# Both attention branches of the second mixer on split fp32r operands, with a smaller key window for one of them and its bias table built elsewhere

## The reference

```python
def neighbourhood_attention(q, k, v, k_ctx, v_ctx, rpb):
    ...
    c0 = np.clip(cols - kc // 2, 0, GRID_W - kc)
    col_idx = (c0[:, None] + np.arange(kc)[None, :]).astype(np.int32)
    ...
        bias = rpb[:, row_off[:, None, None], col_off[None, :, :]].transpose(0, 2, 1, 3)
        s_loc = jnp.einsum('bwhd,brwchd->bhwrc', q_r, k_nb) + bias.astype(q.dtype)
        s_ctx = jnp.einsum('bwhd,bnhd->bhwn', q_r, k_ctx)
        s = jnp.concatenate([s_loc.reshape(B, H, GRID_W, kr * kc), s_ctx], axis=-1)
        p = jax.nn.softmax(s.astype(jnp.float32), axis=-1).astype(q.dtype)
    ...
def gqa_attend(q, k, v):
    s = jnp.einsum('btkgd,bskd->bkgts', q, k)
    p = jax.nn.softmax(s.astype(jnp.float32), axis=-1).astype(q.dtype)
    return jnp.einsum('bkgts,bskd->btkgd', p, v)
```

## Time and profile before

| | |
|---|---|
| median of 3 runs | 3286.6 us (3282.76 to 3290.73) |
| profiled execution, its own time | 3282.52 us |
| its span | 3280.8 us |
| mean granted clock of TensorE | 0.878 |
| busy: PE | 2668.0 us (81%) |
| busy: DVE | 2247.1 us (68%) |
| busy: ACT | 1519.0 us (46%) |
| busy: POOL | 301.4 us (9%) |

### The profile page before, as it was taken

The page is one execution under the profiler, slowest core; times in us unless marked ns, Lnnn a source line. Parts: engine busy times, 40 slices in busy tenths (PEclk is TensorE's granted clock), DMA queues, the critical chain, the costliest instruction groups (busy, mean ns, idle before and its releaser), DMA issues. The chain is left out here.

```text
span 3280.8 us, 38147 instructions
## 1 busy us (share of the span) xinstructions
PE 2668.0 (81%) x12972; PEld 2125.4 (65%) x12972; DVE 2247.1 (68%) x2162; ACT 1519.0 (46%) x1375; POOL 301.4 (9%) x263
## 2 busy tenths in 40 slices
PE   2957965489994499479978359999999999999991
PEld 2844635377773399446657347777787877877771
DVE  5566656378785411356542579999999999999985
ACT  2222120167672323124432136777677776777760
POOL 0100000023321000000000000011111011111110
PEclk9985557599997699789999569999999999999995
DMA  5613511289994322020021159999999999999994
GB/s 205 232 30 141 167 26 59 104 323 371 362 383 172 103 65 95 24 46 1 1 103 52 53 208 355 369 366 359 366 371 366 368 354 366 371 367 366 359 352 147
DMA packets 261961, 732.14 MB, mean 223 GB/s; under 512 B 34995, under 2 KB 75122, under 8 KB 261810
## 3 DMA queue, kind: packets, MB, share of 16 engines
q1 hardware_dynamic: 237394, 654.41, 55.3%
q0 software_dynamic: 19872, 72.39, 5.8%
q10 hardware_dynamic: 4608, 4.20, 0.4%
HBM read 693.16 MB, written 37.80 MB: 223 GB/s over the span
## 5 line engine op out<-in xcount | busy, mean ns | idle before, releaser
L48 PE MATMUL psum_all<-sb_ring_r,sb_arena_r 128*128 128x512 f32 (+1 forms) x2912 | 1071.2, 368 | 0.0
L152 DVE TENSOR_TENSOR sb_ring_r<-sb_ring,sb_hi_ring 128x2048 fp32r<-128x2048 f32 x297 | 674.2, 2286 | 278.8 <-ACT sb_hi_ring L143 273.2
L47 PE MATMUL psum_all<-sb_hi_ring,sb_arena_r 128*128 128x512 f32 (+1 forms) x1880 | 664.8, 354 | 58.0 <-DVE sb_ring_r L152 55.1
L49 PE MATMUL psum_all<-sb_hi_ring,sb_arena_r 128*128 128x512 f32 (+1 forms) x1880 | 659.5, 351 | 0.0
L143 ACT ACTIVATE sb_hi_ring<-sb_ring 128x2048 fp32r<-128x2048 f32 x297 | 564.2, 1914 | 119.4 <-DMA sb_ring<-in_w_gu_dram 36.4
L48 PEld LDWEIGHTS psum_all<-sb_ring_r,sb_arena_r 128*128 128x128 f32 x2912 | 557.4, 191 | 91.6
L152 DVE TENSOR_TENSOR sb_ring_r<-sb_ring,sb_arena_r 128x2048 fp32r<-128x2048 f32 x258 | 581.8, 2283 | 31.0 <-ACT sb_arena_r L143 30.8
L143 ACT ACTIVATE sb_arena_r<-sb_ring 128x2048 fp32r<-128x2048 f32 x258 | 486.2, 1915 | 198.3 <-DMA sb_ring<-in_w_gu_dram 194.0
L47 PEld LDWEIGHTS psum_all<-sb_hi_ring,sb_arena_r 128*128 128x128 f32 x1880 | 359.5, 191 | 114.8 <-DVE sb_ring_r L152 55.7
L47 PE MATMUL psum_all<-sb_arena_r 128*128 128x512 f32 x1032 | 415.2, 402 | 11.9 <-DVE sb_ring_r L152 6.9
L49 PE MATMUL psum_all<-sb_arena_r 128*128 128x512 f32 x1032 | 412.0, 399 | 0.0
(11 more groups left out here) (311 smaller groups left out, 2879.6 us busy)
## 6 DMA issues: line engine op xcount, KB each, us to landing
sb_ring<-in_w_gu_dram SPq DMA_DIRECT2D x272, 1024.0 KB, 6.8
sb_ring<-in_w_dn_dram SPq DMA_DIRECT2D x136, 1024.0 KB, 9.5
sb_ring<-in_w_e_gate_dram SPq DMA_DIRECT2D x36, 1024.0 KB, 7.4
sb_ring<-in_w_e_up_dram SPq DMA_DIRECT2D x36, 1024.0 KB
sb_ring<-in_w_e_down_dram SPq DMA_DIRECT2D x36, 1024.0 KB, 8.1
sb_ring<-in_w_in_dram SPq DMA_DIRECT2D x27, 1024.0 KB, 5.8
sb_ring<-in_w_mod_dram SPq DMA_DIRECT2D x24, 1024.0 KB, 5.8
sb_arena<-in_w_ada_dram POOLq DMA_DIRECT2D x16, 1024.0 KB, 5.6
```

The costliest lines, as they stand in the source:

```text
L47: eng.matmul(out, a[0], b[0], start=start, stop=False)
L48: eng.matmul(out, a[0], b[1], start=False, stop=False)
L49: return eng.matmul(out, a[1], b[0], start=False, stop=stop)
L152: dve.tensor_tensor(s.lo[c % SLOTS], s.raw[c % SLOTS], s.hi[c % len(s.hi)].bitcast(F32), ALU.subtract).then_inc(s.lo_made, 1)
```

## The change

The new function `attend` replaces `attention` for both branches of the second mixer. Heads are now the inner loop: a unit is still one tile of 128 queries and one head, but the 8 heads of a tile follow one another (4 tiles, 32 units in each branch).

- Token order: `turn(..., order=to_grid)` writes the second mixer's tokens in 4 strips of 16 grid columns by 8 rows; `from_grid` brings the result back. A tile of queries is one strip, so NA needs only the strip and its neighbours: 256 grid keys for the outer tiles 0 and 3 (with context 512 in all), 384 for tiles 1 and 2 (640 in all).
- Operands: scores are fp32r products over 128 rows. NA has three (q_hi by k_hi, q_lo by k_hi, q_hi by k_lo), with queries padded by zeros to 128 rows and keys of two heads stacked. GQ has q_hi stacked over q_lo in 128 rows, and two products. Queries and keys are no longer turned in stages tq, tk and tkc but as the `first` fills of `attend`.
- Probabilities are not scaled. They are turned, ACT makes the rounded half (`rounded`), DVE the rest (`rest`, PSUM minus the half), and PE multiplies both by the values: these hold hi and lo beside each other, 128 columns, so a unit has two matmuls of 128 columns for each of its key blocks, and the result is token-major. `put`, once in 4 units, adds the two parts and multiplies by the inverse sums; `o` fills turn a whole tile, from which `rounded` and `rest` write the halves for the output projection. Stage so is gone.
- The bias table: `setup` stores the padded `rpb`; in mod1 ACT issues 128 DMAs from DRAM to DRAM, one for each query position, each of 64 rows of 192 bytes; in `gates_and_lru` SP loads them (1.57 MB) and a mask, POOL adds the mask in 40 `tensor_tensor` of 128 elements on 128 partitions, and SP stores the table (2.6 MB); NA loads it. Stage nb is gone.
- `rotate_heads` works on all 8 heads at a time and ACT makes a second copy of each tile.

The diff at its core:

```diff
+        @block.scalar
+        def _(act):
+            for p in range(P):
+                first = RPB_PAD + (WIN_R - 1 - p // 16) * RPB_C + (WIN_C - 1 - p % 16) - 16
+                src = bass.AP(k.rpb_pad.tensor, first, [[RPB_R * RPB_C, NH], [RPB_C, GRID_H], [1, 48]])
+                act.dma_start(k.rpb_rows[p], src).then_inc(k.rpb_rows_stored, 16)
...
+            pool.wait_ge(s.rows_loaded, 32)
+            for w, first in enumerate((16, 0, 16, 32, 16)):
+                for h in range(NH):
+                    pool.tensor_tensor(table[:, w, h], rows[:, GRID_H * h:GRID_H * (h + 1), first:first + 16],
+                                       wide(window[:, w], 1, GRID_H), ALU.add).then_inc(s.masked, 1)
...
+            sp.wait_ge(k.rpb_rows_stored, 16 * P)
+            sp.dma_start(k.ring[:, 0:2, :].rearrange("p a n -> p (a n)")[:, 0:NH * GRID_H * 48],
+                         k.rpb_rows.rearrange("p m c -> p (m c)")).then_inc(s.rows_loaded, 16)
+            sp.dma_start(k.ring[:, 5, 0:80], a["window_mask"].rearrange("p w c -> p (w c)")).then_inc(s.rows_loaded, 16)
+            sp.wait_ge(s.masked, 5 * NH)
+            sp.dma_start(k.rpb_table, k.ring[:, 2:5, :].rearrange("p a n -> p (a n)")[:, 0:NH * 5 * P]).then_inc(s.table_stored, 16)
+            sp.wait_ge(s.table_stored, 16)
...
+            def fill(m, srcs):
+                if m >= 2:
+                    pe.wait_ge(s.split, m - 1)
+                for i, src in enumerate(srcs):
+                    ins = pe.transpose(k.psum[:, 4 + m % 2, i * P:(i + 1) * P], src, k.ident[:])
+                ins.then_inc(s.turned, 1)
...
+            def score(u):
+                t = u // 8
+                if u % 8 == 0:
+                    hooks.queries_ready(pe, t)
+                    if "queries" in tiles[t] and t > 0:
+                        pe.wait_ge(s.split, at["q", t, 1] + 1)
+                if u == 0 and first:
+                    pe.wait_ge(s.split, len(first))
+                if u >= 2:
+                    pe.wait_ge(s.exp_done, u - 1)
+                for cols, lhs, rhs, start, stop in tiles[t]["products"](u % 8):
+                    ins = pe.matmul(logits[:, u % 2, cols], lhs, rhs, start=start, stop=stop)
+                ins.then_inc(s.scored, 1)
...
+            def turn_probs(u):
+                pe.wait_ge(s.exp_done, u + 1)
+                for i, (g0, g1) in enumerate(parts(u)):
+                    fill(at["p", u, i], [probs[:, u % 2, g * P:(g + 1) * P] for g in range(g0, g1)])
+            def mix(u):
+                pe.wait_ge(s.split, at["p", u, len(parts(u)) - 1] + 1)
+                q = u // 4
+                if u == 0:
+                    hooks.values_ready(pe)
+                if u % 4 == 0 and q >= 2:
+                    pe.wait_ge(s.put, 2 * (q - 1))
+                dst = k.psum[:, 6 + q % 2, (u % 4) * P:(u % 4 + 1) * P]
+                values = tiles[u // 8]["values"](u % 8)
+                for g, v in enumerate(values):
+                    pe.matmul(dst, hi[:, u % 2, g * P:(g + 1) * P], v, start=g == 0, stop=False)
+                    ins = pe.matmul(dst, lo[:, u % 2, g * P:(g + 1) * P], v, start=False, stop=g == len(values) - 1)
+                ins.then_inc(s.mixed, 1)
...
+            for m, group in enumerate(first):
+                fill(m, group["src"])
+            for u in range(STEPS):
+                if u < NU:
+                    score(u)
+                if prepared(u) is not None:
+                    t = prepared(u)
+                    for i in range(2):
+                        fill(at["q", t, i], tiles[t]["queries"](i)["src"])
+                if 1 <= u <= NU:
+                    turn_probs(u - 1)
+                if turned_out(u) is not None:
+                    t = turned_out(u)
+                    pe.wait_ge(s.o_ready, 2 * t + 2)
+                    fill(at["o", t], [otok[:, t % 2, j * P:(j + 1) * P] for j in range(4)])
+                if 2 <= u <= NU + 1:
+                    mix(u - 2)
...
+            def rounded(m, dst, src):
+                act.wait_ge(s.turned, m + 1)
+                act.activation(dst, src, ACT.Copy).then_inc(s.rounded, 1)
+            def exp(u):
+                act.wait_ge(s.max_ready, u + 1)
+                if u >= 2:
+                    act.wait_ge(s.turned, at["p", u - 2, len(parts(u - 2)) - 1] + 1)
+                if u >= 8:
+                    act.wait_ge(s.inverted, u // 4 - 1)
+                n = tiles[u // 8]["n"]
+                act.activation(probs[:, u % 2, 0:n], logits[:, u % 2, 0:n], ACT.Exp, bias=neg_max[:, u % 2:u % 2 + 1],
+                               accum_out=total[:, u % 8:u % 8 + 1]).then_inc(s.exp_done, 1)
...
+            hooks.act(act)
+            for m, group in enumerate(first):
+                rounded(m, group["hi"], bank(m, group["hi"].shape[-1]))
+            for u in range(STEPS):
+                if u < NU:
+                    exp(u)
+                hooks.act_step(act, u, s)
+                if prepared(u) is not None:
+                    for i in range(2):
+                        m = at["q", prepared(u), i]
+                        if i == 0 and prepared(u) >= 2:
+                            act.wait_ge(s.scored, 8 * (prepared(u) - 1))
+                        rounded(m, tiles[prepared(u)]["queries"](i)["hi"], bank(m, 512))
+                if 1 <= u <= NU:
+                    if u - 1 >= 2:
+                        act.wait_ge(s.mixed, u - 2)
+                    for i, (g0, g1) in enumerate(parts(u - 1)):
+                        m = at["p", u - 1, i]
+                        rounded(m, hi[:, (u - 1) % 2, g0 * P:g1 * P], bank(m, (g1 - g0) * P))
+                if turned_out(u) is not None:
+                    m = at["o", turned_out(u)]
+                    dst, view = out(turned_out(u))[0], out(turned_out(u))[2]
+                    rounded(m, dst, view(bank(m, 512)))
...
+            def rest(m, dst, src, half):
+                dve.wait_ge(s.rounded, m + 1)
+                dve.tensor_tensor(dst, src, half.bitcast(F32), ALU.subtract).then_inc(s.split, 1)
+            def find_max(u):
+                t = u // 8
+                dve.wait_ge(s.scored, u + 1)
+                if tiles[t]["bias"] is not None:
+                    part, bias = tiles[t]["bias"](logits[:, u % 2, :], u % 8)
+                    if u == 0:
+                        hooks.bias_ready(dve)
+                    dve.tensor_tensor(part, part, bias, ALU.add).then_inc(s.biased, 1)
+                    dve.wait_ge(s.biased, u + 1)
+                if u >= 2:
+                    dve.wait_ge(s.exp_done, u - 1)
+                dve.tensor_reduce(neg_max[:, u % 2:u % 2 + 1], logits[:, u % 2, 0:tiles[t]["n"]], AX.X, ALU.max,
+                                  negate=True).then_inc(s.max_ready, 1)
+            def put(q):
+                t, at4 = q // 2, 4 * (q % 2)
+                dve.wait_ge(s.mixed, 4 * q + 4)
+                dve.reciprocal(inverse[:, at4:at4 + 4], total[:, at4:at4 + 4]).then_inc(s.inverted, 1)
+                if q:
+                    dve.wait_ge(s.o_ready, q)
+                dve.tensor_copy(tmp, quad(q)[:, :, 0, :]).then_inc(s.put, 1)
+                dve.wait_ge(s.put, 2 * q + 1)
+                dve.tensor_tensor(tmp, quad(q)[:, :, 1, :], tmp, ALU.add).then_inc(s.put, 1)
+                dve.wait_ge(s.put, 2 * q + 2)
+                dve.wait_ge(s.inverted, q + 1)
+                if t >= 2 and q % 2 == 0:
+                    dve.wait_ge(s.turned, at["o", t - 2] + 1)
+                dve.tensor_tensor(otok[:, t % 2, 256 * (q % 2):256 * (q % 2) + 256].rearrange("p (h d) -> p h d", h=4), tmp,
+                                  wide(inverse[:, at4:at4 + 4], 2, HD), ALU.mult).then_inc(s.o_ready, 1)
...
+            hooks.dve(dve)
+            for m, group in enumerate(first):
+                rows = group["rows"]
+                rest(m, group["lo"], k.psum[rows, 4 + m % 2, 0:group["lo"].shape[-1]], group["hi"][rows])
+            for u in range(STEPS):
+                if u < NU:
+                    find_max(u)
+                hooks.dve_step(dve, u, s)
+                if prepared(u) is not None:
+                    for i in range(2):
+                        m = at["q", prepared(u), i]
+                        group = tiles[prepared(u)]["queries"](i)
+                        rest(m, group["lo"], k.psum[group["rows"], 4 + m % 2, 0:512], group["hi"][group["rows"]])
+                if 1 <= u <= NU:
+                    for i, (g0, g1) in enumerate(parts(u - 1)):
+                        m = at["p", u - 1, i]
+                        rest(m, lo[:, (u - 1) % 2, g0 * P:g1 * P], bank(m, (g1 - g0) * P), hi[:, (u - 1) % 2, g0 * P:g1 * P])
+                if turned_out(u) is not None:
+                    m = at["o", turned_out(u)]
+                    dst_hi, dst_lo, view = out(turned_out(u))
+                    rest(m, dst_lo, view(bank(m, 512)), dst_hi)
+                if u >= 6 and (u - 6) % 4 == 0 and (u - 6) // 4 < NU // 4:
```

(39 more changed lines are left out.)

342 lines of the change are left out of this document (227 added, 115 removed).

## The result

The changed kernel takes 3381.07 us (median of 4 runs, 3376.13 to 3386.14) against 3288.66 for the kernel before on the same chip: ratio 1.0279, 95% interval 1.0254 to 1.0305. It is slower by 92 us where 51 were forecast: above the forecast's own 3318 to 3365, inside the stated range of 3280 to 3395.

The account below looks back on a forecast made before the run. PE was taken to bound the old attention branches, a DVE-ACT chain the new ones. Terms -3 + 53 + 2 + 1 - 1 + 1 = +53 on 3282.5 gave 3336, median near 3338; own range 3318 to 3365, stated 3280 to 3395.

Parts of the forecast that it names:

- rival 3: Attention: narrow fp32r matmuls cost what fp32 does, 0.25 us instead of 0.12; +40, total 3378; chance 0.11.
- mod1, +53: mod1: ACT's 128 DMA issues at 0.66 us each end the stage at 100.0 instead of 46.6 us.
- the term between two issues, 0.04: mod1: 0.04 us between ACT's DMA issues, added to 0.62 for each issue.
- Rivals 2 and 5: mod1: 2, cheap issue as L588, +16, 3301, chance 0.13; 5, mod1 keeps its length, 3275 to 3287, chance 0.18.
- Unit time in the attention: NA and GQ: the chain DVE, ACT, ACT, DVE sets units of 3.77 (middle), 3.10 (outer) and 3.58 us (GQ).
- Rival 6: Attention: the chain is shorter than summed and PE is the bound; -75 in place of -3, total 3267; chance 0.09.
- The sum of the attention, -3: NA 144 and GQ 147.5 us, with 1.7 for barriers and the end, against 297.8 for the old stages.
- three `o` turns (1.3: 3.9): Attention loop: turning finished tiles costs 1.3 us each, 3.9 in each branch.
- New queries three times (... 3.6): Attention loop: preparing new queries costs two copies or two rests, 1.2 us each time, 3.6 in each branch.
- rival 4: Attention: PE idles a third of each unit and its clock falls to 1.2 GHz; +118, total 3456; chance 0.07.
- The recurrent stage, +2: Recurrent stage: POOL's table additions are covered, but DVE could be held up 0 to 9 us; +2 taken.
- Small terms: Setup's short stores +1, rotations with fewer, longer instructions -1, ACT's permuted token reads or writes in two turns +1.

Follow-up runs that it names:

- e1_64: Changed kernel with the bias table's rows copied in mod1 by 64 DMAs of 128 rows instead of 128 of 64: 3335.5 us (one run).
- e1_few: Changed kernel with the bias fetched in mod1 by 8 DMAs of long runs (1060 bytes): 3327.4 us, ratio 1.0120 to the kernel before.
- e5: Changed kernel with ACT's rounded copies ahead of the exponential in attend: 3320.9 us, ratio 1.0087 to the kernel before.
- e11: Changed kernel with PE's turn of a finished tile behind the next unit's scores: 3377.2 us, ratio 1.0274 to the kernel before.
- e12: Changed kernel with few DMAs, copies ahead of the exponential, PE warm-up, spread queries and late tile turn: 3225.7 us, ratio 0.9814.
- e2: Changed kernel with DVE's rests of a unit one step later, behind the maximum of the unit after the next: 3491.7 us, ratio 1.0620.

## Why the prediction was right, and where it was off

The direction and the larger of the two terms came out by the mechanism forecast. That 3381 lies near rival 3's 3378 is chance, since its mechanism is out, and it is inside the stated range only because that range was drawn to take in the rivals. Two small slips: 3336 and 4 make 3340 and not 3338, and the attention's terms as listed come to -4.6 and not -3.

- **mod1, +53:** right in mechanism and nearly in size, +60.8. The issue was sized by L714 at 0.62 and took 0.633 in the median; the term between two issues, 0.04, was 0.033. What was missing are the seven long issues beside the weight loads and smaller delays, which make the mean 0.682. e1_64 shows that the number of DMAs sets it, e1_few that the rest of mod1 adds 2 us at most. Rivals 2 and 5 are out; the 326 ns of L588 on the same queue was no guide, nor was the rule of DMA: Bandwidth & Descriptors of the Trainium skill (Issuing engines are not separate DMA queues), that initiation is usually small beside the DMA. For one DMA the traces agree: in e1_64 an issue took 0.62 us and the median landing 2.5. But the landings overlap and the issues of one queue do not, so the 128 issues were the whole stage.
- **Unit time in the attention:** right. Steps of 3.66 and 3.09 in NA and 3.43 in GQ at full clock, against 3.77, 3.10 and 3.58. e5 shows that the order on ACT makes this chain: with the copies ahead a GQ step is 2.7. That is also below the 3.0 that I took for PE's pace in GQ, so that term was too high. Rival 6 (PE sets the pace) is out for the change.
- **The sum of the attention, -3:** wrong, +32.9. The mis-sized terms are "three `o` turns (1.3: 3.9)" and "New queries three times (... 3.6)". I priced the work of these steps and not the bank that `fill` waits for, nor the half clock that follows such a wait; each such step in GQ cost 4.8 us more than a regular one, 28.5 in all for 7.5. That is 21 of the 24 us by which GQ missed its 147.5. In NA, where new queries need no bank, I put down the two copies or the two rests (1.2), while both stand in the chain (2.1 measured). e11 takes 14 us of it back in both branches by PE's order alone. Its start and end were 9 us longer than priced (11.6 to the first exponential and 12.9 from the last, for 8.2 and 7), its regular steps 6 us shorter in all; 3.6 us of both are only one step counted on the other side, as 31 steps lie between the first and the last exponential and the sum has 32.
- **The clock:** rival 4 came true in part, 0.07 chance. In NA the two `o` steps and the query steps account for about 17 us where I had 7.5; steps of 4.9 to 5.7 us in stretches at half clock add some 6. My sum took full clock for granted because both old branches had it. But there PE was busy for 119.6 of 123.4 and 121.9 us and waited over 1 us only four times, at most 1.5, and in the new ones it is busy 75 and 76% of the time, so the old rows said nothing for them. The trace has the order of events, a wait and then the fall. How much of the lost time is the wait itself and how much the clock after it isn't settled: no kernel here changes one alone.
- **Rival 3** is out: narrow fp32r matmuls start 0.11 us apart, near the 0.12 taken.
- **The recurrent stage, +2:** +3.1, which DVE's slower rows beside GpSimd's additions cover in full (3.4). The other kernels with these additions took between 70.7 and 72.5 (69.2 before). The 40 additions took 33.7 us, 0.88 on the mean and 0.632 in the median, and ended at 311.7 of 331: covered, but near the 1.0 us at which the cover ends. GPSIMD Engine Reference of the Trainium skill (Elementwise — side-by-side cycle accounting), twice DVE's time, was nearly right for the median. My 0.20 to 0.29 from a memset and a select were not.
- **Small terms:** setup -0.3 (forecast +1), rotations 0.0 (-1), turns with another token order 0.0 (+1).

## What to carry to other kernels

An idle queue is not free for many small DMAs: count them, not their bytes, and fold rows into runs. Where one engine rounds what another subtracts, write the order of both so that neither stands behind the other's next unit; and price rare steps (a finished tile, new queries) by the buffer that they wait for, not by their work. Lighter matmuls gained nothing here where PE then waits, and lost clock. And a gain of a few us in one execution needs a second execution of the same code beside it.

## What was not expected of the hardware

- The price of an issue did not depend on rows from 64 to 128: 633 and 622 ns. All issues over 1.0 us (seven and nine) came while the weights were loading.
- A DVE instruction of 1.23 us that started during a GpSimd memset of 5.22 us ended 1.1 us after the memset, and so lasted 5.02. One GpSimd addition took 5.9 us where the median is 0.63; DVE's three instructions beside it (a scan and two on 128x2048) were not slower than before.
- Stretches at half clock came where PE was busy 75 and 76% of the changed kernel's two branches, while at 88% and 86% (e12) the mean clock was 0.91 and 0.94; e2's branches, with 2.2 us waits in each unit, had 0.53 and 0.59 at 71 and 74%. These are means of whole branches, and no limit follows from them.
